# Four last tiles of a hybrid decoder layer: norm products of two tiles on GpSimd, partial sums on VectorE, and one pair of output banks at a time

## The reference, cut to what matters

```python
# D_MODEL 1024, BATCH 8, SEQ 4096, one layer; 8 query heads, 2 key/value heads of 64, window 128
h = rmsnorm(x, norm_g)
proj = h @ w_in + b_in                                   # 1024 -> 2816
q, k, v, z_a, u_s, v_s, z_s = split(proj)                # 512,128,128,512,512,512,512
attn = banded_sink_attention(q, k, v, sinks) * silu(z_a) # keys with 0 <= q-k < 128
u_s, v_s = gelu(u_s), gelu(v_s)                          # exact gelu
sgu = u_s * (tril(w_s) @ layernorm(v_s) + b_s) * silu(z_s)   # inside chunks of 128
x = x + concat(attn, sgu) @ w_out + b_out
out = x * rsqrt(mean(x*x) + 1e-5) * final_norm_g         # the final norm
```

## Time and profile before

| What | Value |
|---|---|
| Median of 3 runs | 505.94 us (504.74 to 507.13) |
| Profiled execution, own device time | 506.99 us |
| Span of its slowest core (core 2) | 505.4 us |
| Spans of the other cores | 499.2 to 502.0 us |
| Busy, core 2: TensorE / VectorE / ScalarE / GpSimd | 480.5 / 360.4 / 325.3 / 174.4 us |

### The profile page before, as it was taken

The page is one execution under the profiler, slowest core; times in us unless marked ns, Lnnn a source line. Parts: engine busy times, 40 slices in busy tenths (PEclk is TensorE's granted clock), DMA queues, the critical chain, the costliest instruction groups (busy, mean ns, idle before and its releaser), DMA issues.

```text
span 505.4 us, 9928 instructions; the slowest of 8 cores (499.2 to 505.4 us)
## 1 busy us (share of the span) xinstructions
PE 480.5 (95%) x3260; PEld 238.8 (47%) x3310; DVE 360.4 (71%) x540; ACT 325.3 (64%) x574; POOL 174.4 (34%) x215
## 2 busy tenths in 40 slices
PE   6888999999999899999999999999999999999993
PEld 3763555444444345444454445444454445444442
DVE  2769987775986368774887468873787737965795
ACT  4515866865697636957458675775759655756875
POOL 2004625344405003560245213470143771444122
PEclk9999999999999989999999999999999999999998
DMA  7999799188015922393043753346225421230035
GB/s 216 328 327 334 191 178 337 49 198 281 2 43 119 173 83 86 134 255 113 6 127 119 121 171 128 124 99 193 86 84 169 81 83 45 83 126 0 4 124 209
DMA packets 44403, 71.16 MB, mean 141 GB/s; under 512 B 27584, under 2 KB 27840, under 8 KB 44352
## 3 DMA queue, kind: packets, MB, share of 16 engines
q1 hardware_dynamic: 42912, 68.17, 45.5%
q0 software_dynamic: 1152, 2.10, 2.9%
q10 hardware_dynamic: 288, 0.24, 0.2%
HBM read 49.53 MB, written 16.78 MB: 131 GB/s over the span
## 4 chain that ended last, share of the span: by engine, by line
PE 82%; DMA 7%; DVE 4%; issue 3%; ACT 2%; SPq 1%; POOLq 0%; POOL 0%; DVEq 0%; ACTq 0%
PE pp L583 41%; PE pp L869 19%; PE pp L658 10%; DMA xe<-w_in 5%; PE pp L802 3%; PE pp L627 3%; PE pp L747 2%; DMA xT<-xn 2%; PE pp L752 1%; PE pp L703 1%; PE pp L797 1%; DVE w_all L516 1%; ACT ET L758 1%; SPq L487 0%; DVE vs_f L663 0%
## 5 line engine op out<-in xcount | busy, mean ns | idle before, releaser
L583 PE MATMUL pp<-xT,w_all 128*128 128x512 bf16 x1024 | 232.6, 381 | 6.3 <-DMA xT<-xn 2.0
L583 PEld LDWEIGHTS pp<-xT,w_all 128*128 128x128 bf16 x1056 | 101.5, 98 | 126.9 <-issue 8.5
L869 PE MATMUL pp<-w_out_bf,mixT 128*128 128x512 bf16 (+1 forms) x503 | 114.1, 376 | 1.7 <-issue 1.2
L856 POOL TENSOR_TENSOR xe<-xe,bout_sb 128x1024 f32<-128x1024 f32 x28 | 67.1, 2398 | 50.3 <-DVE ET L771 26.3
L869 PEld LDWEIGHTS pp<-w_out_bf,mixT 128*128 128x128 bf16 x520 | 49.6, 98 | 58.1 <-issue 2.5
L758 ACT ACTIVATE ET<-pp 128x1536 bf16<-128x1536 f32 x32 | 46.6, 1455 | 22.8 <-PE pp L752 22.8
L883 POOL TENSOR_SCALAR st_fm<-st_fs 128x1 f32<-128x1 f32 x28 | 7.9, 283 | 142.9 <-ACT junk L881 142.3
L710 DVE SCALAR_TENSOR_TENSOR sgt<-pp,pack_b_sb,Cmat 128x512 f32<-128x512 f32 x32 | 23.7, 748 | 40.3 <-PE pp L703 38.0
L658 PE MATMUL pp<-w_all,xT 128*128 128x512 bf16 x224 | 51.8, 379 | 0.2 <-DVE xT L561 0.2
L873 DVE TENSOR_TENSOR xe<-pp,xe 128x512 f32<-128x512 f32 x56 | 38.3, 685 | 18.6 <-PE pp L869 18.4
L881 ACT ACTIVATE junk<-xe 128x1024 bf16<-128x1024 f32 x28 | 29.8, 1064 | 26.6 <-DVE xe L873 26.5
(11 more groups left out here) (89 smaller groups left out, 602.8 us busy)
## 6 DMA issues: line engine op xcount, KB each, us to landing
xa<-x SPq DMA_DIRECT2D x32, 512.0 KB, 7.0
xe<-x SPq DMA_DIRECT2D x28, 512.0 KB, 3.7
out<-xe SPq DMA_DIRECT2D x28, 512.0 KB, 2.7
xe<-w_in SPq DMA_DIRECT2D x12, 512.0 KB, 12.8
mixT<-w_in SPq DMA_DIRECT2D x10, 512.0 KB, 15.1
w_out_bf<-w_out POOLq DMA_DIRECT2D x8, 256.0 KB, 8.9
out<-w_all SPq DMA_DIRECT2D x4, 256.0 KB, 2.2
LR<-sgu_wT SPq DMA_DIRECT2D x1, 512.0 KB, 16.9
```

The costliest lines, as they stand in the source:

```text
L583: ins = e.matmul(bank(h), lhsT=w_all[:, cb, k, :], rhs=xT[:, xb, k, :], start=(k == 0), stop=(k == 7))
L856: G.op("pool", lambda e: e.tensor_tensor(out=buf[:, s, :], in0=buf[:, s, :], in1=bout[:], op=ALU.add), reads=["c_bout"], writes=[key], cos ...
L869: ins = e.matmul(bank(h)[:, 0:width], lhsT=mixT[:, mb, ec, tt * 128:(tt + 1) * 128], rhs=w_out[:, ec, cols], start=(ec == 0), stop=(ec == 7))
```

## The change

Four things change.

1. The last four tiles. The table `LAST` goes. Tiles 28 and 29 (`LAST_APART`) now use the ordinary path with two differences: the root is taken on ScalarE by Ln and Exp (`root`), and the norm factor product with the weights (y*g) is made ahead, by GpSimd in two halves into a freed part of w_all; one instruction of 1024 columns, on ScalarE for tile 28 and on VectorE for tile 29, then multiplies in the row's factor. Before, tile 28 had one VectorE instruction for it all, and tiles 29 and 30 had their products on GpSimd and their scaling split between VectorE and ScalarE. Tile 30 now has the ordinary path, and its VectorE scaling is held back (`hold`) until the last residual add and the last partial sum of tile 31 are through. Tile 31 keeps its parts of 512, 256 and 256 columns; columns 0 to 511 go by GpSimd product and ScalarE scaling, the rest by one VectorE instruction. The partial sums of squares, ScalarE steps of 128x1 (L900) in each of the four tiles before, are two VectorE steps of 128x1, in tile 31 alone; the other three tiles take their sum of squares in one instruction of 1024 columns. All last stores are issued by SyncE.
2. The two root steps, Ln and Exp, are put directly behind each other (`lead`).
3. `CAPS["V"]` goes from 4 to 2: PV of a block is not placed before the pair of banks of the block ahead is free.
4. `SEEDS` change for stages 0, 2 and 6.

```diff
-LAST = {4: ((512, 512), (None, None), 0), 3: ((512, 512), ("pool", "pool"), 512), 2: ((512, 512), ("pool", "pool"), 512),
-        1: ((512, 256, 256), ("dve", "dve", "dve"), 640)}
-SEEDS = (33433, 300, 13108, 300, 300, 300, 300, 63561)
+LAST_PARTS = (512, 256, 256)
+LAST_APART = {NT - 4: "act", NT - 3: "dve"}
+SEEDS = (61899, 300, 300, 300, 300, 300, 70729, 63561)
...
-    CAPS = {"S": 3, "V": 4, "P": 4, "Q": 4}
+    CAPS = {"S": 3, "V": 2, "P": 4, "Q": 4}
...
+            if n in LAST_APART:
+                root(n, st_fs[:, s:s + 1], eps_t[:, 0:1], [("fs", s), "eps"], v1)
...
+            if n in LAST_APART:
...
+                for hf in range(2):
+                    cols = slice(hf * 512, (hf + 1) * 512)
+                    G.op("pool", lambda e, cols=cols: e.tensor_tensor(out=src[:, cols], in0=buf[:, s, cols], in1=gf[:, cols], op=ALU.mult),
+                         reads=[key + (hf,), "c_gf"], writes=[old[hf]], cost=1.25, prio=v1, port=True)
+                by = {"act": (1.1, lambda e: e.activation(out=src, in_=src, func=AF.Copy, scale=st_fr[:, s:s + 1])),
+                      "dve": (0.95, lambda e: e.tensor_scalar(out=src, in0=src, scalar1=st_fr[:, s:s + 1], scalar2=None, op0=ALU.mult))}
...
+        def root(n, sq, bias, reads, prio):
+            s = n % 4
+            o = None
+            for kw in (dict(in_=sq, func=AF.Ln, scale=1.0 / D, bias=bias), dict(in_=st_fr[:, s:s + 1], func=AF.Exp, scale=-0.5)):
+                o = G.op("act", lambda e, kw=kw: e.activation(out=st_fr[:, s:s + 1], **kw), reads=reads, writes=[("fr", s)], cost=0.38, prio=prio,
+                         phase=3 * (NS - 1) + PH_EXP, lead=o)
...
-                G.op("act", lambda e: e.activation(out=rest, in_=sq, func=AF.Identity, scale=1.0 / D, bias=rest if i else eps_t[:, 0:1]),
-                     reads=[("ms", par, i), "eps"], writes=[("fm", s)], cost=0.2, prio=v0 - 0.5)
+                last_rest.append(G.op("dve", lambda e: e.tensor_scalar(out=rest, in0=sq, scalar1=1.0 / D, scalar2=rest if i else EPS, op0=ALU.mult, op1=ALU.add),
+                                      reads=[("ms", par, i)], writes=[("fm", s)], cost=0.12, prio=v0 - 0.8))
...
+            hold[0].after += (last_add[-1], last_rest[-1])
```

More of the change, by code:

```diff
@@ L887, in out_tile @@
-            G.op("dve", lambda e: e.scalar_tensor_tensor(out=buf[:, s, :], in0=buf[:, s, :], scalar=st_fr[:, s:s + 1], in1=gf[:],
-                                                         op0=ALU.mult, op1=ALU.mult),
-                 reads=[("fr", s), "c_gf"], writes=both, cost=1.3, prio=v1, port=True)
-            G.op("sp", lambda e: e.dma_start(out=out_d[n * 128:(n + 1) * 128, :], in_=buf[:, s, :]),
-                 reads=both, writes=[key], cost=0.5, dsem=d_xa[s] if last else d_xe[s], kb=512, prio=v0, final=True)
@@ L893, in finish_part @@
-        def finish_part(n, y, mem, key, old, v0, i, cols, width, final, by):
+            if n in LAST_APART:
+                root(n, st_fs[:, s:s + 1], eps_t[:, 0:1], [("fs", s), "eps"], v1)
+            else:
+                G.op("pool", lambda e: e.tensor_scalar(out=st_fm[:, s:s + 1], in0=st_fs[:, s:s + 1], scalar1=1.0 / D, scalar2=EPS,
+                                                       op0=ALU.mult, op1=ALU.add), reads=[("fs", s)], writes=[("fm", s)], cost=0.19, prio=v1, port=True)
+                G.op("pool", lambda e: e.tensor_tensor(out=st_fr[:, s:s + 1], in0=st_fm[:, s:s + 1], in1=nh[:, 0:1], op=ALU.pow),
+                     reads=[("fm", s), "nh"], writes=[("fr", s)], cost=0.57, prio=v1, port=True)
@@ new lines, in out_tile @@
+            src = buf[:, s, :]
+            if n in LAST_APART:
+                cb = CB_U + 2 * (NT - 1 - n)
+                src, old = w_all[:, cb:cb + 2, :, :].rearrange("p a k c -> p (a k c)").bitcast(F32), [("w", cb), ("w", cb + 1)]
+                for hf in range(2):
[4 more added lines that the diff above has]
+                      "dve": (0.95, lambda e: e.tensor_scalar(out=src, in0=src, scalar1=st_fr[:, s:s + 1], scalar2=None, op0=ALU.mult))}
+                G.op({LAST_APART[n]: by[LAST_APART[n]]}, None, reads=[("fr", s)], writes=old, prio=v1, port=True)
+                G.op("sp", lambda e: e.dma_start(out=out_d[n * 128:(n + 1) * 128, :], in_=src), reads=old, cost=0.5, dsem=d_xa[s], kb=512,
+                     prio=v0, final=True)
+                return
@@ new lines, in out_tile @@
+            o = G.op("dve", lambda e: e.scalar_tensor_tensor(out=src, in0=src, scalar=st_fr[:, s:s + 1], in1=gf[:], op0=ALU.mult, op1=ALU.mult),
+                     reads=[("fr", s), "c_gf"], writes=both, cost=1.3, prio=v1, port=True)
+            if n == NT - 2:
+                hold.append(o)
+            G.op("sp", lambda e: e.dma_start(out=out_d[n * 128:(n + 1) * 128, :], in_=src), reads=both, writes=[key], cost=0.5,
+                 dsem=d_xa[s] if last else d_xe[s], kb=512, prio=v0, final=True)
@@ new lines, in finish_end @@
+        def finish_end(n, y, key, v0, parts):
+            s = n % 4
+            mem = w_all[:, CB_U, :, :].rearrange("p k c -> p (k c)").bitcast(F32)
+            G.op("pool", lambda e: e.tensor_tensor(out=mem, in0=y[:, 0:512], in1=gf[:, 0:512], op=ALU.mult), reads=[key + (0,), "c_gf"],
+                 writes=[("w", CB_U)], cost=1.2, prio=v0 - 0.5, port=True)
+            G.op("act", lambda e: e.activation(out=mem, in_=mem, func=AF.Copy, scale=st_fr[:, s:s + 1]), reads=[("fr", s)],
+                 writes=[("w", CB_U)], cost=0.7, prio=v0 - 0.6)
+            both = [key + (i,) for i in range(1, parts)]
+            G.op("dve", lambda e: e.scalar_tensor_tensor(out=y[:, 512:], in0=y[:, 512:], scalar=st_fr[:, s:s + 1], in1=gf[:, 512:],
+                                                         op0=ALU.mult, op1=ALU.mult),
+                 reads=[("fr", s), "c_gf"], writes=both, cost=0.75, prio=v0 - 0.6, port=True)
+            rows = out_d[n * 128:(n + 1) * 128, :]
+            for cols, src, need in ((slice(0, 512), mem, [("w", CB_U)]), (slice(512, D), y[:, 512:], both)):
+                G.op("sp", lambda e, cols=cols, src=src: e.dma_start(out=rows[:, cols], in_=src), reads=need, cost=0.35,
+                     dsem=sem(f"d_end{cols.start}"), kb=256, prio=v0, final=True)
+            hold[0].after += (last_add[-1], last_rest[-1])
```

52 lines of the change are left out of this document (11 added, 41 removed).

## The result

| kernel, first study | us, median (lowest to highest) | runs |
|---|---|---|
| before | 505.25 (503.92 to 507.13) | 13 |
| changed | 509.75 (508.07 to 513.35) | 13 |

The account below looks back on a forecast made before the run. The prediction took TensorE's matmul stream as the bound, with core 2's stall setting the time. Span 502.0 + 0.5 + 0.6 - 0.4 - 0.6 = 502.1, plus 1.6 around it: 503.7 us, range 501.9 to 507.2.

Parts of the forecast that it names:

- The stall of stage 3: First Q group on core 2: 2.04 us waiting for a late transpose plus a half-clock group, 3.6 us, would go.
- The metric is then the slowest core without a stall, 502.0: With core 2 at 501.8, core 5, which had no stall, would set the span at 502.0 us.
- The opening: Start of the kernel: nearly the same TensorE rows in both programs, so counted at nothing, 1 us either way.
- The V cap: Stages 0, 1 and 7: PV stands behind the mixT of the block ahead; 0.5 us lost.
- rival C: Slower, 510.2 us: with a 6.5 us chain, seven PVs in stages 0, 1 and 7 wait 0.9 each; chance 0.11.
- The chain from a PV to its mixT: From the end of the last PV to the end of its mixT, taken as 5.1 us.
- Only VectorE's scaling beside a product on GpSimd was priced: At the last tiles, a VectorE instruction beside a GpSimd product takes 1.99 instead of 1.28 us: +0.7.
- Tile 31's wait: Last tiles: with fewer matmuls as cover, TensorE waits 0 to 1.3 us for mixT, counted as 0.6.
- The end: Behind TensorE's last matmul: 0.8 us won, half given back to the stores; -0.4, between -1.1 and +0.4.
- old waits dropped: Waits for mixT and folds that the new order drops: -0.6 us; core 5 had 0.9 on mixT alone.
- The signs: Right: no stage 3 transpose wait, full clock, spans within 3 us; wrong: PV waits, another late Q group, no shorter end.
- Rival B: The gain is lost in another core or place, one core late again: 505 to 506.5 us; chance 0.21 with D, no gain.

Follow-up runs that it names:

- e8: The changed kernel with only the seed of stage 0 set back to 33433: ratio to before 1.0066.
- e6: The changed kernel with GpSimd's output bias add reduced to 8 of 1024 columns for tiles 0 to 3: ratio to before 1.0083.
- e5: The changed kernel with the seeds of before, keeping the tail code and V cap of 2: ratio to before 1.0022.
- the cut: GpSimd's output bias add reduced to 8 of 1024 columns, for all 32 tiles: ratio 1.0023 in the changed kernel, 0.9969 in the kernel before.
- after2: The changed kernel measured once more without an edit, on another group's chip: ratio to before 1.0043.
- two cuts: The changed kernel with all bias adds at 8 columns and stage 2's squares not waiting for x: ratio 0.9965 with both, 1.0023 and 1.0083 singly.

## Why the prediction was wrong, point by point

- *The stall of stage 3 goes, 3.6 us on core 2*: right that it goes. Its size is 3.4: the 3.27 us of the slow group are a timeline row, and a group of 8 takes 1.89 in such rows; 1.73 is its pitch. In the mean over the cores the stretch won 1.2 us (1.7 to 0.5 in the table), of which 0.4 are waits at 132 to 137 us for mixT, a fold and an Exp, and not the stall. That the other cores' loads make a transpose land late was argued in the prediction and stays so: no run here separates it.
- *The metric is then the slowest core without a stall, 502.0*: wrong in what it assumed, that the rest of the order costs the same. The changed order has, by the stretches below, some 5 us more of waits on TensorE, of which stall and end give back 2.3.
- *The opening is counted at nothing, 1 us either way*: mis-sized; it costs 1.1 us (e8, and the waits for zsT and for the transposes' bank), and 2.0 by the profiled runs of e6 and e8, which are of one chip. I had compared the rows of TensorE's list, and not what its banks wait for on ScalarE and VectorE.
- *The V cap: PV stands behind the mixT of the block ahead, 0.5 us; rival C with seven PVs waiting 0.9 each*: the mechanism is wrong. The cap is a rule for the order that the scheduler plans; on the chip a PV waits only for those who used the banks that it was given, and there are other pairs. On core 5 the PV at 83.29 starts 2.95 us before the end of the mixT product of the block ahead, L833:

```profile
83.29 0.30 PE L797 MATMUL pp<-PT,v_r 64*64 64x256 bf16 x4
...
85.56 0.68 DVE L833 TENSOR_TENSOR mixT<-pp,LR 128x512 bf16<-128x512 f32 x1
```

No PV waits behind 60 us in the changed kernel's two profiled runs but one, 0.47 on one core. What waits is the output group: 1.54 and 0.75 us in stage 1 of e5. I looked at the instruction that the cap holds back and not at those that move up beside it.
- *The chain from a PV to its mixT takes 5.1 us*: this was read from one block, the last. In stage 1 it takes 8.6 on core 5 (the PV that ends at 84.16 has its mixT at 92.73) and was up to 9.8 before. Rival C's condition, 6.5, was met, and the wait fell on another instruction than C said: the output groups, 0.90 for mixT.
- *Only VectorE's scaling beside a product on GpSimd was priced, at the tail, +0.7*: this is the step that failed most plainly. I had the row of 1.28 growing to 1.99 beside GpSimd and thought of it for the new products at the end, while 32 adds of 2.4 us already lay on GpSimd and every new order puts other VectorE work beside them. By the table the cut takes back 1.5 us in stage 1 (and 0.6 in before) and 1.4 in stage 6 (nothing in before). By the mean spans, whose runs differ in their openings, the adds are 0.8 of the 3.0 us, and the squares behind late x loads, for which the sum had no term, 1.2 once the adds are gone.
- *Tile 31's wait, 0.6*: right, 0.48 to 0.49 on every core.
- *The end, -0.4 net, 0.8 won and half given back*: it was 1.0 to 1.1 shorter, the favourable bound of my range; its square starts 0.16 us behind its add (forecast 0.3).
- *0.6 us of old waits dropped*: wrong; that for L771 (0.9) went and larger ones came.
- *The signs*: no Q group of another stage behind a transpose, no PV waits at several blocks, a shorter end, and a granted clock of 1.00 from 150 to 480 us on all cores. Only the spans, 3.8 us apart where I had said 3, spoke against the forecast. None of the three signs of being wrong named the way in which it was wrong.

By size, in the mean of the two profiled runs: opening 1.2, stage 1 1.4, stage 6 1.3, the last stretch with tile 31 0.8, other stretches 0.4, less 1.2 for the stall and 1.1 for the end: 2.8. The spans' means differ by 3.7 (505.1 and 501.4), 0.8 of which lies ahead of the first v_s group (25.0 and 24.2 us), where both lists are alike; in after2's group it was 3.0. Rival B named the kind of outcome (time lost in another place) but sized it as a lucky or unlucky core, where all but the bank wait sits on all of them.

## What to carry to other kernels

When a list is reordered as a whole, an instruction list of one engine says nothing of the price: check, stage by stage, which engine frees the buffer that the bound engine needs next, and what runs beside it. Where VectorE and GpSimd share work, price each GpSimd instruction as a possible stop of VectorE wherever the new order puts it, not only at the new ones. If a removed cost yields nothing, look for a second one at the same place before dropping the theory: two cuts here gave 2.0 us and nothing alone, and 3.3 together, in the mean span. And read a chain from the stage that it is used for: the same one took 5.1 us at the end and 8.6 in stage 1.
